# Second mixer reordered on ScalarE and VectorE, one key turn a quarter later, the last weightings spread over two tiles

## The reference

```python
def mixer_c(n, w_in, gq, gk, w_out):
    q, k, v = _split(n @ w_in, (C_WIDTH, C_WIDTH, C_WIDTH))      # 1024 each, 8 heads of 128
    q = rmsnorm(q.reshape(bsz, s_len, N_HEADS_C, HEAD_DIM), gq)
    k = rmsnorm(k.reshape(bsz, s_len, N_HEADS_C, HEAD_DIM), gk)
    return stick_breaking(q, k, v).reshape(bsz, s_len, C_WIDTH) @ w_out

def stick_breaking(q, k, v):      # per head; mask: key before query
    z = einsum('bthd,bshd->bhts', qb, k) * d_h ** -0.5
    lo = where(mask, log_sigmoid(-z), 0.0)
    rc = cumsum(lo, axis=3, reverse=True)
    a = where(mask, exp(log_sigmoid(z) + (rc - lo)), 0.0)
    return einsum('bhts,bshd->bthd', a, v)
```

## Time and profile before

| | us |
|---|---|
| runs: median, lowest, highest of 3 | 1006.18, 1003.8, 1006.38 |
| the profiled execution | 1006.29 |
| its span, first to last instruction | 1004.5 |
| TensorE busy | 979.2 |
| VectorE, ScalarE, GpSimd busy | 593.7, 530.3, 351.7 |
| TensorE clock granted over the span, as a share of full speed | 0.993 |

### The profile page before, as it was taken

How to read it: one execution, slowest core, us unless ns; L and a number is a source line. 1 busy time by engine, 2 the same in 40 slices (tenths; PEclk the granted TensorE clock), 3 DMA queues, 4 the chain that set the end, 5 groups by cost and what they waited for, 6 DMA issues and landing times.

```text
span 1004.5 us, 15002 instructions
## 1 busy us (share of the span) xinstructions
PE 979.2 (97%) x6302; PEld 885.1 (88%) x6302; DVE 593.7 (59%) x803; ACT 530.3 (53%) x717; POOL 351.7 (35%) x109
## 2 busy tenths in 40 slices
PE   7999999999999999999999999999999899999997
PEld 6888889999888887779999888799999899999885
DVE  4897946788321535436888312445218579888643
ACT  6676346555333566546555333545453678566432
POOL 0011045565656554345565666354540000000000
PEclk9999999999999999899999999999999999999999
DMA  9454224555555452434554555344444426555531
GB/s 336 164 180 155 84 92 163 195 181 174 204 198 178 168 209 84 156 100 167 181 196 168 207 174 205 139 176 160 168 168 168 168 95 212 182 191 183 187 149 42
DMA packets 24807, 168.51 MB, mean 168 GB/s; under 512 B 2781, under 2 KB 3092, under 8 KB 4900
## 3 DMA queue, kind: packets, MB, share of 16 engines
q1 hardware_dynamic: 24452, 167.22, 46.7%
q10 hardware_dynamic: 288, 0.33, 0.1%
HBM read 166.49 MB, written 1.05 MB: 167 GB/s over the span
## 4 chain that ended last, share of the span: by engine, by line
PE 91%; DVE 4%; ACT 3%; issue 1%; DMA 1%; SPq 0%; DVEq 0%; ACTq 0%
PE bank L637 28%; PE bank L638 27%; PE bank L639 27%; PE bank L830 2%; ACT whi L1121 1%; DVE wlo L1671 1%; PE bank L665 1%; DMA h<-x_rows 1%; PE bank L923 0%; PE bank L798 0%; PE bank L847 0%; PE bank L1039 0%; PE bank L1023 0%; PE bank L866 0%; PE bank L940 0%
## 5 line engine op out<-in xcount | busy, mean ns | idle before, releaser
L2312 POOL TENSOR_TENSOR wlo<-raw,whi 128x1024 fp32r<-128x1024 f32 (+1 forms) x102 | 350.6, 3439 | 384.6 <-ACT whi L1121 377.0
L1671 DVE TENSOR_TENSOR wlo<-raw,whi 128x1024 fp32r<-128x1024 f32 (+2 forms) x152 | 246.8, 1624 | 307.2 <-ACT whi L1121 307.0
L1121 ACT ACTIVATE whi<-raw 128x2048 fp32r<-128x2048 f32 (+1 forms) x154 | 292.9, 1903 | 150.7 <-PE bank L639 149.6
L637 PE MATMUL bank<-nhi,whi 128*128 128x256 f32 (+3 forms) x840 | 241.2, 287 | 4.5 <-DVE nlo L2198 3.2
L638 PE MATMUL bank<-nlo,whi 128*128 128x256 f32 (+3 forms) x840 | 238.5, 284 | 0.0
L639 PE MATMUL bank<-nhi,wlo 128*128 128x256 f32 (+3 forms) x840 | 238.0, 283 | 0.0
L637 PEld LDWEIGHTS bank<-nhi,whi 128*128 128x128 f32 (+1 forms) x840 | 160.4, 191 | 8.4 <-issue 8.3
L639 PEld LDWEIGHTS bank<-nhi,wlo 128*128 128x128 f32 (+1 forms) x840 | 160.6, 191 | 0.0
L638 PEld LDWEIGHTS bank<-nlo,whi 128*128 128x128 f32 (+1 forms) x840 | 160.5, 191 | 0.1
L637 PE MATMUL bank<-mhi,whi 128*128 128x258 f32 x384 | 109.3, 285 | 1.7 <-DVE mlo L2146 1.0
L638 PE MATMUL bank<-mlo,whi 128*128 128x258 f32 x384 | 108.4, 282 | 0.0
(11 more groups left out here) (283 smaller groups left out, 1547.3 us busy)
## 6 DMA issues: line engine op xcount, KB each, us to landing
raw<-w_stream SPq DMA_DIRECT2D x154, 1024.0 KB, 4.8
cst<-consts SPq DMA_DIRECT2D x1, 1200.0 KB, 11.2
h<-x_rows SPq DMA_DIRECT2D x4, 256.0 KB, 5.3
raw<-w_stream SPq DMA_DIRECT2D x2, 512.0 KB, 6.4
out_rows<-e SPq DMA_DIRECT2D x4, 256.0 KB, 2.0
e<-g_post SPq DMA_DIRECT2D x1, 512.0 KB, 3.5
raw<-w_stream SPq DMA_DIRECT2D x1, 352.0 KB, 9.1
b<-consts_x SPq DMA_DIRECT2D x1, 272.0 KB
```

Source lines behind the costliest of these rows:

```text
L637: pe.matmul(out, lhsT.hi, rhs.hi, start=start, stop=False)
L1121: act.activation(whi[j][:, 0:n], raw[j][:, 0:n], ACT.Copy).then_inc(s_hi.up(i))
L1671: dve.tensor_tensor(wlo[j][:, 0:m], raw[j][:, 0:m], whi[j][:, 0:m].bitcast(F32), ALU.subtract).then_inc(s_lod.up(i))
L2312: pool.tensor_tensor(wlo[j][:, m:n], raw[j][:, m:n], whi[j][:, m:n].bitcast(F32), ALU.subtract).then_inc(s_lop.up(i))
```

## The change

There are four edits, all for the second mixer.

- `cut`: tiles 50 to 66 are now wholly VectorE's; GpSimd has none of them.
- `STICKS`: turn 3 moves from quarter (10, 1) to (10, 2); scores 4 and 5 both stand in (10, 3); weightings 6 and 7 move from the second output tile to the third.
- `normed`: the sum per head is taken by ScalarE's accumulator, with four squares of 128 columns in place of one of 512, and VectorE's reduction goes.
- The lists of ScalarE and VectorE: turn 3 ahead of `shares(3)` and `hi(C0 + 11)`; `log_share(2)` ahead of `lo(C0 + 10)`; `hi(C0 + 13)` and `lo(C0 + 13)` some steps later.

```diff
 def cut(i):
-    return n if i < OUT_AB + 2 or i >= FOURIER + 2 else n // 2
+    return n if i < OUT_AB + 2 or C0 - 1 <= i < OUT_C + 4 or i >= FOURIER + 2 else n // 2
 STICKS
-    (10, 1): [("sr", 3), ("cT", 3)],
-    (10, 2): [("sz", 4)],
-    (10, 3): [("sz", 5)],
+    (10, 1): [("sr", 3)],
+    (10, 2): [("cT", 3)],
+    (10, 3): [("sz", 4), ("sz", 5)],
-    ("out", 1): [("sv", 4), ("sv", 5), ("sv", 6), ("sv", 7)],
+    ("out", 1): [("sv", 4), ("sv", 5)],
+    ("out", 2): [("sv", 6), ("sv", 7)],
 ScalarE, normed
-                    act.activation(QN[:, i % 4, :], u.t[:, :], ACT.Square, scale=rc[:, tt:tt + 1]).then_inc(s_csq.up(i))
-                    on.wait_ge(*s_css.at(i))
-                    inv_rms_row(small[:, 148 + 4 * i:152 + 4 * i], 2, tt, s_crs.up(i))
+                    ss = small[:, 148 + 4 * i:152 + 4 * i]
+                    for hd in range(4):
+                        act.activation(QN[:, i % 4, hd * P:hd * P + P], u.t[:, hd * P:hd * P + P], ACT.Square, scale=rc[:, tt:tt + 1],
+                                       accum_out=ss[:, hd:hd + 1]).then_inc(own.up())
+                    on.wait_ge(*own.last())
+                    inv_rms_row(ss, 2, tt, s_crs.up(i))
 ScalarE, order
             shares(2)
-            hi(C0 + 11)
-            shares(3)
             turn(3, 0)
             turn(3, 1)
+            shares(3)
+            hi(C0 + 11)
             log_term(4)
+            values(0)
             log_term(5)
-            values(0)
             hi(C0 + 12)
             log_term(6)
-            hi(C0 + 13)
             shares(4)
             log_term(7)
             cat_hi(1, "sv", 0)
             shares(5)
+            hi(C0 + 13)
             cat_hi(1, "sv", 1)
 VectorE, normed
-                    on.wait_ge(*s_csq.at(i))
-                    dve.tensor_reduce(ss, qv, AX.X, ALU.add).then_inc(s_css.up(i))
 VectorE, order
             normed(3)
+            log_share(2)
             lo(C0 + 10)
-            log_share(2)
             log_share(3)
+            masked(4)
             lo(C0 + 11)
-            masked(4)
+            log_sum(4)
             masked(5)
-            log_sum(4)
...
             masked(7)
-            lo(C0 + 13)
             log_share(5)
             log_sum(7)
             cat_lo(1, "sv", 0)
+            cat_lo(1, "sv", 1)
             log_share(6)
-            cat_lo(1, "sv", 1)
             log_share(7)
+            lo(C0 + 13)
             cat_lo(1, "sv", 2)
             cat_lo(1, "sv", 3)
```

More of the change, by code:

```diff
@@ L606, in block_kernel @@
         s_ffhi, s_fflo = sig("ffhi", grid(2, 16)), sig("fflo", grid(2, 16))
-        s_gs, s_csq, s_css, s_crs = sig("gs", [0]), sig("csq", range(8)), sig("css", range(8)), sig("crs", range(8))
+        s_gs, s_crs = sig("gs", [0]), sig("crs", range(8))
         s_sln, s_sll, s_sa = (sig(n, range(8)) for n in ("sln", "sll", "sa"))
```

## The result

| | us |
|---|---|
| changed, median of 7 runs (lowest, highest) | 1009.57 (1008.3, 1010.45) |
| before, median of 7 runs beside it (lowest, highest) | 1004.33 (1003.8, 1006.38) |
| ratio, with its 95% interval | 1.0048 [1.0036, 1.0059] |
| profiled execution of the changed kernel | 1009.57, span 1007.8 |

The forecast was 1006.2 with a range to 1008.2. The time lies above the range, and 5.2 us above the kernel before, which is clear of the noise and on the side that the forecast held least likely.

The account below looks back on a forecast made before the run. With TensorE busy 979.2 of 1004.5 us, only its waits and low-clock stretches could move the time. 1006.29 plus 0.6 of waits less 0.65 of clock gave 1006.2 us, range 1002.9 to 1008.2.

Parts of the forecast that it names:

- turn 3: TensorE's wait at the scores of head 4, behind the evacuation of turn 3, goes: -2.9 us.
- hand-over: Entry to the second mixer: the wider lo of tile 52 delays the additions to h, without slack: +1.1 us.
- key sums 2: Key sums 2: two wider lo, 2.1 us, in the chain of their log sum against 1.55 slack: +0.5 us.
- weighting 3: Weighting 3: lo of tile 64 now stands ahead of cat_lo of head 2 on VectorE: +2.2 us, wait 3.2.
- weightings 6 and 7: Moving these weightings to the third output tile costs and brings nothing: 0 us.
- clock, turn 3: The low clock stretch behind turn 3's wait goes with that wait: -2.95 us.
- clock, weighting 3: The clock falls behind the 3.2 us wait at weighting 3, priced between 1.7 and 2.95: +2.3 us.
- A rule against the row: VectorE's instructions slowed beside GpSimd, together 3.1 us, were taken as made up off the path: 0 counted.
- two of two: Both earlier TensorE waits of this length, 2.87 and 3.2 us, were followed by a low clock stretch.
- The rival that no fall follows: The wait moves to weighting 3 but the clock does not fall with it: 1003.9 us, chance 0.14.
- VectorE relieved: Rival: VectorE's time regained from GpSimd is on the path, no new long wait or fall: 1001.7 us, chance 0.10.
- VectorE too late, slower: Rival: turn 3's slack fails, scores 4 wait 2 us and the clock falls there too: 1010.5 us, chance 0.08.

Follow-up runs that it names:

- Experiments 1 and 2: Changed kernel with weightings 6 and 7 back beside 4 and 5, 1005.36 us; or only hi and lo of tile 66 before evacuating heads 6 and 7, 1005.41 us.
- experiment 10: The kernel before with one edit, weightings 6 and 7 in the third output tile in place of the second: 1004.37 us, ratio 1.0001 to before.
- experiment 9: Changed kernel with full cut only from tile 53, weightings 6 and 7 with 4 and 5, lo of tile 64 behind cat_lo of head 2: 1000.77 us.
- Experiment 3: The changed kernel with tiles 67 and 68 also given wholly to VectorE: 1007.53 us, ratio 1.0023 to before.
- the split kernel: The kernel before with only weightings 6 and 7 moved to the third output tile: 1004.37 us; it was profiled twice.
- experiment 6: The changed kernel with the full cut only from tile 53, not from 50: 1007.49 us, ratio 1.0024 to before.
- experiment 4: The changed kernel with lo of tile 64 one step later on VectorE, behind cat_lo of head 2: 1004.47 us, ratio 0.9998 to before.
- experiment 11: The kernel before with one edit, VectorE doing the whole of tiles 50 to 66: 1009.11 us, ratio 1.0041 to before.

## Why the prediction was wrong

Each term, by the trace:

| term | forecast | measured |
|---|---|---|
| turn 3 | -2.9 | -2.87 |
| hand-over | +1.1 | +1.02 |
| key sums 2 | +0.5 | +0.18 |
| norms, turn 2 | +0.2 | +0.15 |
| key sums 7 | -0.5 | -0.45 |
| weighting 3 | +2.2 | +2.20 |
| weightings 6 and 7 | 0 | **+2.17** |
| sum of the waits | +0.6 | +2.4 |
| clock, turn 3 | -2.95 | -2.95 |
| clock, weighting 3 | +2.3 | +2.45 |
| clock, second hand-over | 0 | **+1.7** |

By these the trace should be 3.6 us longer. The span is 3.3 longer, with a start-up 0.3 shorter: the transposes of the first layer's hand-over begin at 152.3 in the changed kernel and at 152.6 in the one before.

**The step that failed** is "Moving weightings 6 and 7 costs and brings nothing: TensorE does the same steps, and their inputs are there." It looked at TensorE's inputs. It did not look at what is queued on ScalarE and VectorE behind what the moved steps release: `cat_hi` and `cat_lo` of heads 6 and 7, then `hi` and `lo` of tiles 66 to 68, then the additions to `h`, then the transposes of the hand-over. Experiments 1 and 2 take the wait away, once on TensorE and once in the two lists, and experiment 10 makes a smaller one in the kernel before. The step was put at 0 and measured 2.17 us of wait and 1.7 us of clock. With it the forecast would have been 3.9 us higher, 1010.1, against 1009.57 measured.

**A second part of the same step** is "A rule against the row", where I counted nothing for GpSimd. I asked only what VectorE gains in the stretch that GpSimd leaves, and there nothing is right (experiment 9). But the cut goes back to half at tile 67, and with a full `lo` of 66 in front VectorE comes to its half of 67 0.36 us behind GpSimd. Experiment 3 puts this at 1.3 us of the 2.17, and the fall of the clock with it. The Trainium skill, SBUF — State Buffer, section "Who interferes with whom", has this too: "Issue order, not op shape, decides who blocks." The rows here agree, 1.23 us for VectorE when it starts first and 3.42 when it doesn't. I had read the section for the exclusion alone.

**The baseline.** The sum was made against the profiled execution, 1006.29, which lay beside a median of 1006.18 from three runs. Over more runs the median of before is 1004.3, and the profile belongs to the dearer third. The remaining 1.9 us between the traces' 3.3 and the medians' 5.2 come from there. It hid 1.9 us of what the change costs against before, and is not why the measured time lies above 1006.2. What the cheaper two thirds look like inside was not seen for this kernel; that the clock stays up behind a 2.87 us wait in some executions was, in the split kernel. So "two of two" was a thin ground for taking each fall as sure and -2.95 as its size. The rival that no fall follows is not a different mechanism but one outcome of the same wait, seen in one execution of five at 2.87 us.

**What was right.** Turn 3: the slack held, and alone it is worth 5.8 us in the trace, 3.8 by the medians. The hand-over has no slack, and a wider `lo` comes out whole (experiment 6). Weighting 3 waits for all of `lo` 64 (experiment 4), and the clock falls there. That the 2.3 us put down for this fall met the 2.45 of the first profile is in part luck: in the second it cost 1.6 (15.40 less 13.80). Key sums 2 was mis-sized, 0.5 forecast and 0.18 measured: the two wider `lo` are 2.1 us, and the slack took up all but 0.2 of them. Of the rivals, "VectorE relieved" is refuted by experiment 9. "VectorE too late, slower" gave nearly the right time at the wrong place: scores 4 did not wait, though experiment 11 shows that they would have without the move.

## What to carry to other kernels

When a step is moved on the busy engine, follow what its end releases on the other engines, and everything that stands behind that in their lists, up to the next point at which the busy engine waits; a step whose own inputs are there can still make another late. Widen one engine's share of a copy only where nothing waits behind it, and look at the tile where the share goes back, since the order in which the two engines start there decides which of them is late. And hold a profile against many runs before its clock is put into a sum.

## What the runs showed of the hardware

- The granted clock fell with TensorE waits of 2.12, 2.17, 2.87, 3.18, 3.2 and 4.4 us, and with none of up to 1.2. At 2.87 us it fell in three executions of before and in one of the split kernel, and stayed at 1.00 in another of the split kernel. Between the program's first 15 us and its last 6 every low stretch was 3.4 or 6.8 us long.
- Two half copies started together on VectorE and GpSimd, 128x1024 each, took 1.23 and 3.44 us with VectorE ahead by 0.05, and 3.42 and 2.70 with GpSimd ahead by 0.36. A full one on VectorE alone takes 2.29. So a half beside GpSimd can be slower than the whole without it.
- The start-up differs between executions: the transposes of the first layer's hand-over begin between 151.5 and 153.0 us in the eighteen profiles, whose kernels are the same up to there, and between 152.6 and 153.0 in the three of the kernel before.
